# A normalised sum's factor taken after the matrix product, and additions in four-tile operations, in a two-block transformer layer

## The reference

```python
x = x + rmsnorm(y, g_post_mix[l])                       # y = merged @ w_o
h = rmsnorm(x, g_pre_mlp[l])
f = jnp.square(jax.nn.relu(jnp.einsum('bsd,df->bsf', h, w_up[l])))
f = jnp.einsum('bsf,fd->bsd', f, w_down[l])
x = x + rmsnorm(f, g_post_mlp[l])
...                                                     # second block
u = rmsnorm_2(h, mix_norm_w[l])
p = u @ w_in[l]                                         # 4096 + 16 + 3328 columns: dn, gab, rw
...
def rmsnorm_2(x, w):
    xf = x.astype(jnp.float32)
    y = xf * lax.rsqrt(jnp.mean(xf * xf, axis=-1, keepdims=True) + RMS_EPS)
    return (y * w.astype(jnp.float32)).astype(x.dtype)
```

## Time and profile before

| | us |
|---|---|
| median of 3 runs | 3041.54 (3038.80 to 3041.58) |
| the profiled execution's own time | 3038.55 |
| its span | 3036.8 |
| PE busy in the span | 2865.1 (94%) |
| DVE busy | 2007.7 (66%) |
| ACT busy | 1439.6 (47%) |
| POOL busy | 133.8 (4%) |

### The profile page before, as it was taken

How to read it: one execution, slowest core, us unless ns; L and a number is a source line. 1 busy time by engine, 2 the same in 40 slices (tenths; PEclk the granted TensorE clock), 3 DMA queues, 4 the chain that set the end, 5 groups by cost and what they waited for, 6 DMA issues and landing times.

```text
span 3036.8 us, 51454 instructions
## 1 busy us (share of the span) xinstructions
PE 2865.1 (94%) x19508; PEld 2504.6 (82%) x19508; DVE 2007.7 (66%) x2534; ACT 1439.6 (47%) x1857; POOL 133.8 (4%) x149
## 2 busy tenths in 40 slices
PE   7999999998999999999899899588979999999997
PEld 6888888877888888887788788477767888888886
DVE  6798887767646565565876665753758657566665
ACT  4545656554444444444558433533536444444443
POOL 3000000230000000001000000000102000000001
PEclk9999999999999999999899999799989999999998
DMA  5655554755666666665355444001535655666664
GB/s 190 188 187 174 179 161 146 228 161 161 190 189 188 188 187 189 188 189 182 111 168 169 122 119 119 22 3 37 163 101 178 189 187 185 191 189 189 187 187 132
DMA packets 481998, 486.66 MB, mean 160 GB/s; under 512 B 14912, under 2 KB 479808, under 8 KB 481840
## 3 DMA queue, kind: packets, MB, share of 16 engines
q1 hardware_dynamic: 480288, 478.55, 51.0%
q0 software_dynamic: 1552, 5.93, 0.6%
HBM read 481.28 MB, written 3.15 MB: 160 GB/s over the span
## 4 chain that ended last, share of the span: by engine, by line
PE 43%; DVE 6%; ACT 2%; issue 1%; DVEq 0%; POOLq 0%; POOL 0%; ACTq 0%
PE pg L428 24%; PE pg L435 12%; PE p L975 1%; PE p L989 1%; PE p L992 1%; DVE lo L343 1%; PE p L1348 1%; DVE rw_xx L1041 0%; ACT hi L307 0%; DVE half L682 0%; DVE xa L632 0%; DVE dnc L1076 0%; PE p L1589 0%; DVE work L2077 0%; PE p L1109 0%
## 5 line engine op out<-in xcount | busy, mean ns | idle before, releaser
L343 DVE TENSOR_TENSOR lo<-raw,hi 128x1024 fp32r<-128x1024 f32 x900 | 1092.0, 1230 | 732.7 <-ACT hi L307 728.5
L307 ACT ACTIVATE hi<-raw 128x1024 fp32r<-128x1024 f32 x900 | 942.7, 1058 | 1112.4 <-PE pg L435 1093.7
L428 PE MATMUL pg<-xa,hi 128*128 128x512 f32 x4224 | 1074.8, 396 | 16.4 <-DVE xa L666 14.2
L428 PEld LDWEIGHTS pg<-xa,hi 128*128 128x128 f32 x4224 | 764.2, 190 | 161.7 <-issue 21.8
L428 PE MATMUL pg<-xb,hi 128*128 128x512 f32 x3008 | 767.9, 398 | 31.4 <-DVE xb L487 15.6
L428 PEld LDWEIGHTS pg<-xb,hi 128*128 128x128 f32 x3008 | 548.0, 191 | 134.8 <-issue 17.0
L435 PEld LDWEIGHTS pg<-xa,lo 128*128 128x128 f32 x4224 | 577.5, 191 | 42.6 <-DVE lo L343 0.7
L435 PE MATMUL pg<-xa,lo 128*128 128x256 f32 x4224 | 589.7, 282 | 0.3 <-DVE lo L343 0.3
L435 PEld LDWEIGHTS pg<-xb,lo 128*128 128x128 f32 x3008 | 412.0, 191 | 34.5 <-DVE lo L343 4.9
L435 PE MATMUL pg<-xb,lo 128*128 128x256 f32 x3008 | 421.3, 283 | 2.7 <-DVE lo L343 2.7
L317 ACT ACTIVATE half<-pg 128x512 f32<-128x512 f32 x220 | 128.4, 583 | 90.2 <-PE pg L435 85.8
(11 more groups left out here) (400 smaller groups left out, 1764.2 us busy)
## 6 DMA issues: line engine op xcount, KB each, us to landing
raw<-w_in SPq DMA_DIRECT2D x264, 512.0 KB, 4.6
raw<-ffn_w SPq DMA_DIRECT2D x256, 512.0 KB, 4.3
raw<-w_up SPq DMA_DIRECT2D x128, 512.0 KB, 3.9
raw<-w_down SPq DMA_DIRECT2D x128, 512.0 KB, 4.4
raw<-w_o SPq DMA_DIRECT2D x32, 512.0 KB, 4.9
raw<-w_out SPq DMA_DIRECT2D x32, 512.0 KB, 3.6
raw<-w_sb_out SPq DMA_DIRECT2D x16, 512.0 KB, 4.6
raw<-w_conv_out SPq DMA_DIRECT2D x16, 512.0 KB, 4.5
```

The source lines that it names most:

```text
L307: nc.scalar.activation(hi[:, slot], raw[:, slot], ACT.Copy).then_inc(hi_ready, 1)
L343: nc.vector.tensor_tensor(lo[:, slot], raw[:, slot], hi[:, slot].bitcast(F32), ALU.subtract).then_inc(lo_ready, 1)
L428: nc.tensor.matmul(pg[:, par, t, :], lhsT=hi[:, slot, k, c:c + P], rhs=g.x[:, kk, :], start=(j == 0 and k == 0), stop=False)
```

## The change

Norms 2 and 4 are treated as the late projections are: `xa` is written from the residual times the gain, and the factor `rs` multiplies the results. So `w_up`'s four products take the form of relu2 with a factor (one more DVE operation a block, 32 blocks), and `dn`, `gab` and `rw` change from "store" to "normed" (one more a block, 30 blocks). Norms 2 and 4 are no longer summed on PE: ACT squares four tiles at once into `work`, and DVE folds the 16 tiles into one with five additions (`fold_dve`).

The residual additions are done for four tiles at once. ACT multiplies each tile of the result by its gain in place (`y_act`), DVE multiplies four tiles by `rs` (`y_scale_dve`), and the addition of quarters 0 and 2 is DVE's, of quarters 1 and 3 POOL's. POOL does the memory's squares in pairs, so that it is through with them earlier. The steps stand at other slabs than before.

```diff
+            up = Gemm(plan, f"up{p}", a["w_up"], D, p * D, D, xa, "relu2", (xb, 0, 0), norm=2)
...
-            if g.norm is None:
-                nc.vector.scalar_tensor_tensor(out=sq[:, :, :], in0=sq[:, :, :], scalar=0.0, in1=sq[:, :, :],
-                                               op0=ALU.max, op1=ALU.mult).then_inc(squared, 1)
-            else:
-                norm_rs_dve(dve, g.norm)
-                nc.vector.scalar_tensor_tensor(out=sq[:, :, :], in0=sq[:, :, :], scalar=0.0,
-                                               in1=rs[:, None, :].to_broadcast([P, 2, T]), op0=ALU.max,
-                                               op1=ALU.mult).then_inc(scaled, 1)
-                dve.wait_ge(scaled, own_sq - ff2[0].sq0)
-                nc.vector.tensor_tensor(sq[:, :, :], sq[:, :, :], sq[:, :, :], ALU.mult).then_inc(squared, 1)
+            norm_rs_dve(dve, g.norm)
+            nc.vector.scalar_tensor_tensor(out=sq[:, :, :], in0=sq[:, :, :], scalar=0.0,
+                                           in1=rs[:, None, :].to_broadcast([P, 2, T]), op0=ALU.max,
+                                           op1=ALU.mult).then_inc(scaled, 1)
+            dve.wait_ge(scaled, own_sq)
+            nc.vector.tensor_tensor(sq[:, :, :], sq[:, :, :], sq[:, :, :], ALU.mult).then_inc(squared, 1)
             dve.wait_ge(squared, own_sq)
...
 
-        POOLED = (0, 1, 3, 5, 6, 7)
+        POOLED = tuple(range(8))
...
+        YS = 16
+        y4 = lambda q: work[:, YS + 4 * q:YS + 4 * q + 4, PAD:COLS]
+        resid4 = lambda q: resid[:, 4 * q:4 * q + 4]
+
+        def y_act(act, e, n, k, weight):
+            square_tile(act, n, k, work, PAD, YS)
+            y = work[:, YS + k, PAD:COLS]
+            nc.scalar.activation(y, y, ACT.Copy, scale=weight(k)).then_inc(y_weighted, 1)
+
+        def y_beside_act(act, g, e, n, weight):
+
+            def after(m):
+                if m:
+                    act.wait_ge(evacuated, g.b0 + m + 2)
+                    for k in (2 * m - 2, 2 * m - 1):
+                        y_act(act, e, n, k, weight)
+            return after
+
+        def y_rest_act(act, g, e, n, weight):
+            act_link(nc.scalar.activation(small[:, 140:141], const("ones")[:, 0:1], ACT.Ln))
+            blocks_out(act, g)
+            for k in (DT - 2, DT - 1):
+                y_act(act, e, n, k, weight)
+
+        def y_scale_dve(dve, e, q, n):
             norm_rs_dve(dve, n)
-            for k in range(DT + 1):
-                if k and k % 2 == 0:
-                    yield
-                if k < DT:
-                    if k >= 2:
-                        dve.wait_ge(norm_res, DT * added + k - 1)
-                    seq["dve"] += 1
-                    nc.vector.scalar_tensor_tensor(out=tmp[:, k % 2], in0=work[:, tile0 + k, PAD:COLS],
-                                                   scalar=gain(k), in1=rs[:, :], op0=ALU.mult,
-                                                   op1=ALU.mult).then_inc(dve_seq, 1)
-                if k:
-                    dve.wait_ge(dve_seq, seq["dve"] - (1 if k < DT else 0))
-                    nc.vector.tensor_tensor(resid[:, k - 1], resid[:, k - 1], tmp[:, (k - 1) % 2],
-                                            ALU.add).then_inc(norm_res, 1)
-
+            dve.wait_ge(y_weighted, DT * e + 4 * q + 4)
+            nc.vector.tensor_tensor(y4(q), y4(q), rs[:, None, :].to_broadcast([P, 4, T]), ALU.mult).then_inc(y_ready, 1)
+
+        def y_add_dve(dve, e, q):
+            dve.wait_ge(y_ready, 4 * e + q + 1)
+            nc.vector.tensor_tensor(resid4(q), resid4(q), y4(q), ALU.add).then_inc(added_dve, 1)
+
+        def y_add_pool(pool, e, q):
+            pool.wait_ge(y_ready, 4 * e + q + 1)
+            nc.gpsimd.tensor_tensor(resid4(q), resid4(q), y4(q), ALU.add).then_inc(added_pool, 1)
+
+        def wait_added(eng, e, q):
+            eng.wait_ge(added_pool if q % 2 else added_dve, 2 * e + q // 2 + 1)
+
+        def next_act(act, e, n, q, weight):
+
+            wait_added(act, e, q)
+            for k in range(4 * q, 4 * q + 4):
+                nc.scalar.activation(xa[:, k, 0:T], resid[:, k], ACT.Copy, scale=weight(k)).then_inc(norm_hi, 1)
+            nc.scalar.activation(y4(q), resid4(q), ACT.Square).then_inc(norm_sq, 4)
+
+        def next_dve(dve, m, q, weight):
+            for k in range(4 * q, 4 * q + 4):
+                gained_dve(dve, m, weight, k)
+
+        def fold_dve(dve, e, n):
+
+            dve.wait_ge(norm_sum, POOLED.index(n))
+            steps = [(y4(0), y4(0), y4(q)) for q in range(1, 4)]
+            steps += [(work[:, YS:YS + 2, PAD:COLS], work[:, YS:YS + 2, PAD:COLS], work[:, YS + 2:YS + 4, PAD:COLS])]
+            for i, (o, x, y) in enumerate(steps):
+                if i < 3:
+                    dve.wait_ge(norm_sq, DT * n + 4 * i + 8)
+                if i:
+                    dve.wait_ge(folded, 4 * e + i)
+                nc.vector.tensor_tensor(o, x, y, ALU.add).then_inc(folded, 1)
+            dve.wait_ge(folded, 4 * e + 4)
+            nc.vector.tensor_tensor(sq_sum[:, :], work[:, YS, PAD:COLS], work[:, YS + 1, PAD:COLS], ALU.add).then_inc(norm_used, DT)
+
...
-        g_dn = Gemm(plan, "dn", w2in, D, 0, 4096, xa, "store", (work, DQ, PAD))
-        g_gab = Gemm(plan, "gab", w2in, D, 4096, BW, xa, "store", (work, GA, PAD), apart=DN_H)
-        g_rw = Gemm(plan, "rw", w2in, D, 4112, 3328, xa, "store", (work, RR, PAD))
+        g_dn = Gemm(plan, "dn", w2in, D, 0, 4096, xa, "normed", (work, DQ, PAD), norm=4)
+        g_gab = Gemm(plan, "gab", w2in, D, 4096, BW, xa, "normed", (work, GA, PAD), apart=DN_H, norm=4)
+        g_rw = Gemm(plan, "rw", w2in, D, 4112, 3328, xa, "normed", (work, RR, PAD), norm=4)
...
-            norm_pool(pool, 1, lambda k: mem_pool(pool, k))
+            def mem_pairs(k):
+                if k < DT // 2:
+                    mem_pool(pool, 2 * k)
+                    mem_pool(pool, 2 * k + 1)
+            norm_pool(pool, 1, mem_pairs)
+            for q in (1, 3):
+                y_add_pool(pool, 0, q)
             blocks_out(pool, g_mv)
             pool.dma_start(a["kv"], work[:, 0:8, PAD:COLS]).then_inc(kv_out, 16)
             norm_pool(pool, 3)
+            for q in (1, 3):
+                y_add_pool(pool, 1, q)
...
             def post_mix():
-                norm_act(act, 1, work, PAD, 16, lambda e, k: blocks_out(e, g_wo), DT - 2)
+                y_rest_act(act, g_wo, 0, 1, post_mix_w)
+                yield
+                yield
+                norm_root(act, 1)
                 mem_root_act(act)
                 yield
                 yield
-                yield
-                yield from norm_act_steps(act, 2, resid, 0, 0, lambda e, k: e.wait_ge(norm_res, k + 1))
+                for q in range(4):
+                    next_act(act, 0, 2, q, pre_mlp_w)
+                    yield
+                yield from skip(4)
+                norm_root(act, 2)
+                yield
...
-            norm_split_act(act, 1, xa)
...
-                gemm_act(act, g, squares_beside(act, g, 3, work, PAD, 16) if g is ff1[-1] else None, follows=n)
-            norm_act(act, 3, work, PAD, 16, lambda e, k: blocks_out(e, ff1[-1]), DT - 2)
-            norm_act(act, 4, resid, 0, 0, lambda e, k: e.wait_ge(norm_res, DT + k + 1))
-            norm_split_act(act, 2, xa)
+                gemm_act(act, g, y_beside_act(act, g, 1, 3, post_mlp_w) if g is ff1[-1] else None, follows=n)
+            y_rest_act(act, ff1[-1], 1, 3, post_mlp_w)
+            norm_root(act, 3)
+            for q in range(4):
+                next_act(act, 1, 4, q, mix_w)
+
+            def mix_root():
+                yield from skip(3)
+                norm_root(act, 4)
+                yield
...
-            gemm_act(act, g_dn, conv_l2, follows=g_gab)
+            gemm_act(act, g_dn, conv_l2, follows=g_gab, each=step_of(mix_root()))
...
             def post_mix():
-                yield
-                yield
-                yield from norm_add_steps(dve, 1, 0, 16, lambda k: v1("g_post_mix", k), work[:, ADD_TMP:ADD_TMP + 2, PAD:COLS])
+                yield from skip(3)
+                y_scale_dve(dve, 0, 0, 1)
+                y_add_dve(dve, 0, 0)
+                yield
+                y_scale_dve(dve, 0, 1, 1)
+                y_scale_dve(dve, 0, 2, 1)
+                yield
+                y_add_dve(dve, 0, 2)
+                y_scale_dve(dve, 0, 3, 1)
+                yield
+                for q in range(4):
+                    next_dve(dve, 1, q, pre_mlp_w)
+                    yield
+                fold_dve(dve, 0, 2)
+                yield
...
-            blocks_out(dve, g_mv)
-            norm_rs_dve(dve, 2)
-            norm_split_dve(dve, 1, xa, resid, 0, 0, lambda k: v1("g_pre_mlp", k), 80)
...
-            norm_add_dve(dve, 3, 1, 16, lambda k: v1("g_post_mlp", k))
-            norm_rs_dve(dve, 4)
-            norm_split_dve(dve, 2, xa, resid, 0, 0, lambda k: v2("mix_norm_w_2", k), 96)
+            y_scale_dve(dve, 1, 0, 3)
```

(32 more changed lines are left out.)

22 lines of the change are left out of this document (8 added, 14 removed).

## The result

The changed kernel takes 3029.19 us (median of 6 runs, 3028.44 to 3031.71). The kernel before, beside it, takes 3041.56 us (6 runs, 3038.8 to 3043.05). The ratio is 0.9962, with a 95% interval of 0.9950 to 0.9974: 0.4% faster. Forecast were 3034 us and a range of 3026 to 3043, with "faster" as the likeliest outcome.

What follows compares the result with a forecast made beforehand. PE was taken as the bound in the feed-forward, with waits at norms and dn's block turn nearly PE's block. 11 - 3.5 - 0.7 = 6.8 us gained gave 3031.8 profiled, some 3034 against the median; range 3026 to 3043.

Steps and rivals of the forecast that it cites:

- The extra operation, 0.73 us: Each of 62 evictions takes DVE 0.73 us more: free in up, 0.7 us charged in rw, counting in dn.
- First place, steps 1 and 2: mem_k to up0: norm 1's total and root, ACT back at slabs at 662.0, DVE's first products done by 670.7.
- Step 3, POOL's addition: mem_k to up0: POOL's addition of four tiles takes 2.4 us, bounds 0.73 and 6.9.
- Steps 4 to 6: mem_k to up0: ACT's copies, DVE's fold until 699.4, PE waiting 3 to 7 us, up0 at 707.4; gain 11.
- Second place, start: down3 to dn: dn's first slab starts at 1452.7 instead of 1464.61, 11.9 us earlier.
- What is left of it at block 2: In dn, ACT reaches block 2's slabs at 1483.4 against 1484.61 before, so 11.9 us have become 1.2.
- The turns: dn's ACT, DVE, ACT turn per block becomes 11.49 us, and 15.86 with the l2 norm, against PE's 11.2.
- The clock behind the last wait: In dn, slabs after a long PE wait run at the lower clock; 3 us more if behind the last one.
- POOL beside DVE: Rival, chance 0.25: POOL's additions don't hold DVE, block 2's slabs in dn come 4.7 us earlier; 3030 us.
- The upper bound of the first place: mem_k to up0: a gain of 12 us if POOL's addition takes only 0.73 us.
- Given back: Rival, chance 0.21: POOL's additions take 4 us or more and PE runs at the lower clock; sum near 0, 3041 us.
- The eviction is on the bound everywhere: Rival, chance 0.06: in dn, gab and rw each of 30 evictions costs 0.73 us, 21.9 in all; 3052 us.

Runs made afterwards that it cites:

- up_plain: Changed kernel with the old one-operation eviction in the four up products, norm 2's factor left out there; 3029.64 us.
- gab_rw_store: Changed kernel with one-operation evictions again in gab and rw only, norm 4's factor left out there; 3031.22 us.
- dn_store: Changed kernel with dn's 16 blocks evicted in one operation, norm 4's factor and the wait for its root left out there; 3021.16 us.
- dve_adds: Changed kernel with all four parts of the residual additions on DVE, none on POOL; 3025.97 us.

## Why the prediction was right

The sign, the place of the gain and, in the main, the mechanism of both places were right, and the time lay in the range, 4.8 us under the forecast. Step by step:

- **The extra operation, 0.73 us.** Right, and right in where it counts. The `up` blocks: 0 (up_plain). `rw` and `gab`: 0 (gab_rw_store); I had charged 0.7 us. `dn`: all of it (dn_store, 8.0 us in time).
- **First place, steps 1 and 2.** ACT is back at slabs at 663.04, 15.0 us behind `mem_k`'s start; forecast were 15.4.
- **Step 3, POOL's addition.** 2.38 and 2.52 us where it ran undisturbed, 2.4 taken. The one that met a running product took 3.33, as a short one did in the earlier trace rows.
- **Steps 4 to 6.** Norm 2's total 50.9 us behind `mem_k`'s start, forecast 52.8; the wait there 5.78 us within the 3 to 7; `up0` at 59.7, forecast 60.8. A quarter of `xa`'s rest took DVE 1.66 us each time where the sum has 1.92, and ACT's four copies with their square 2.65 where it has 2.85. So 12.4 us gained instead of 11.
- **Second place, start.** 13.0 us earlier, forecast 11.9.
- **What is left of it at block 2.** This size was off: 4.3 us instead of 1.2. Of the 3.1 us between, 1.1 come from the start and 0.6 from the slabs up to the total; 1.4 are norm 4's root. I let it load two tables behind the total. The first load (at 1459.12) was done ahead of the total (1460.57), so only one stands in the chain.
- **The turns.** Forecast 11.49 and 15.86 us, measured 11.48 and 15.85. So ACT's last l2 turn came at 186.2 us behind `down3`'s end instead of 189.4, the same 3.1 us again.
- **The clock behind the last wait.** Named with 3 us "if this falls behind the last long wait"; it did, and cost 1.5. The sum of 3.5 carried the 3.0 us of ACT and 0.5 of this. Together with ACT's -0.2 that is +1.3 instead of +3.5.

The Trainium skill's rule on shared access (SBUF — State Buffer, "Who interferes with whom") held at the longer size: DVE's two-input operations waited out a whole addition of four tiles. Its GPSIMD Engine Reference ("Elementwise — side-by-side cycle accounting") gave an estimate of 2.3 us for such an addition by halving, and the undisturbed ones took 2.38 and 2.52.

"POOL beside DVE" falls by the 3.43, 3.23 and 3.75 us above and by dve_adds, though its time (3030) was nearer than mine: the 4.7 us that it gave to additions beside DVE came in part from the root's table load, an earlier start and an eviction in `rw` that costs nothing, so its nearness is luck.

The sum itself gives 3031.8 in the profiled execution's terms and 3034.8 against the median, of which 3034 is a rounding down; the median is 5.6 us under it. Of these, 2.5 are the terms above (9.3 gained in the profiled executions, 6.8 in the sum): 1.4 at the first place, 2.2 at the second, 0.4 in what lies behind, less the 1.4 us by which the profiled execution was late before `mem_k`, which were chance. The other 3.0 are the step from the profiled execution to the median: I added what before's runs show, but the changed kernel's profiled execution (3029.23) lies at its median. The upper bound of the first place is a slip: by the sum's own steps an addition of 0.73 us makes the chain 1.7 us shorter, so 13 and not 12.

"Given back" falls: the first place kept all of its gain, and POOL's addition is 2.4 and not 4 us. "The eviction is on the bound everywhere" falls by gab_rw_store, and holds in `dn` alone.

## What to carry to other kernels

Whether a short operation on a half idle engine costs anything is decided by the turn it stands in: write down the turn (who hands to whom until the next block's first step) and hold it against the bound engine's block; 0.7 us were free in 46 evictions, and cost 8 us in the 16 of `dn`. An earlier start is worth only what the next such turn leaves of it, so look for the gain at the last wait behind it, not at the start. When a factor is moved to the eviction, its total may be fetched inside the next product: here that gave 5.3 us more.
